# Twelve modulation products, a sooner first load and another order of the first rows in a two-block layer

## Time and profile before

| | us |
|---|---|
| median of 3 runs | 1569.6 |
| lowest and highest | 1567.91 and 1569.87 |
| the profiled execution's own time | 1573.47 |
| its span | 1571.5 |
| PE busy | 1459.9 (93%) |
| DVE busy | 1049.8 (67%) |
| POOL busy | 563.6 (36%) |
| ACT busy | 546.4 (35%) |
| DMA moved | 571.91 MB, mean 364 GB/s |

### The profile page before, as it was taken

The page is one execution under the profiler, slowest core; times in us unless marked ns, Lnnn a source line. Parts: engine busy times, 40 slices in busy tenths (PEclk is TensorE's granted clock), DMA queues, the critical chain, the costliest instruction groups (busy, mean ns, idle before and its releaser), DMA issues.

```text
span 1571.5 us, 22748 instructions
## 1 busy us (share of the span) xinstructions
PE 1459.9 (93%) x8272; PEld 1120.8 (71%) x8272; DVE 1049.8 (67%) x2170; ACT 546.4 (35%) x1128; POOL 563.6 (36%) x382
## 2 busy tenths in 40 slices
PE   8999999999999999999999999998988988888777
PEld 7999998767999999998989985444444443333333
DVE  6655376875734328998976468785858585858556
ACT  5444353363544436443134242221212121212114
POOL 2455428220344441001002234554545444444451
PEclk9999999999999999999999999999999998999999
DMA  9888958996999997999976969999999999999996
GB/s 365 312 329 317 348 217 338 315 326 241 407 372 371 376 376 294 374 398 342 362 281 226 401 244 403 404 427 427 427 427 426 427 427 427 427 427 427 426 428 267
DMA packets 99814, 571.91 MB, mean 364 GB/s; under 512 B 11536, under 2 KB 11664, under 8 KB 50448
## 3 DMA queue, kind: packets, MB, share of 16 engines
q1 hardware_dynamic: 61056, 298.15, 51.3%
q0 software_dynamic: 37520, 268.47, 40.7%
q10 hardware_dynamic: 1152, 4.16, 0.7%
HBM read 569.67 MB, written 135.27 MB: 449 GB/s over the span
## 4 chain that ended last, share of the span: by engine, by line
PE 57%; DMA 26%; DVE 6%; SPq 5%; POOL 3%; issue 2%; ACT 1%; ACTq 0%; POOLq 0%; DVEq 0%
DMA arena<-pairs,eidx 15%; PE ps L2727 10%; PE ps L2113 8%; PE ps L2112 8%; PE ps L2111 8%; DMA ring<-pairs,eidx 6%; PE ps L2504 5%; SPq L664 3%; PE ps L2200 2%; PE ps L2198 2%; PE ps L2199 2%; DMA arena<-in_ada 2%; POOL w_lo L754 2%; SPq L663 2%; PE ps L2619 2%
## 5 line engine op out<-in xcount | busy, mean ns | idle before, releaser
L2727 PE MATMUL ps<-arena 128*128 128x512 f32 x844 | 402.6, 626 | 69.1 <-ACT arena L1252 69.1
L2727 PEld LDWEIGHTS ps<-arena 128*128 128x128 f32 x844 | 165.8, 201 | 289.0 <-issue 192.8
L1965 DVE CUSTOM_DVE_ANT_0 arena<-arena 128x1024 f32<-128x1024 f32 x211 | 255.2, 1225 | 145.3 <-DMA arena<-pairs,eidx 144.1
L822 POOL DMA_INDIRECT arena<-pairs,eidx x210 | 244.3, 1163 | 257.1 <-PE ps L2727 208.4
L754 POOL TENSOR_TENSOR w_lo<-ring,w_hi 128x1024 fp32r<-128x1024 f32 x76 | 207.9, 2738 | 257.7 <-DVE w_lo L1305 171.3
L2111 PE MATMUL ps<-u_hi,w_hi 128*128 128x256 f32 (+1 forms) x912 | 259.4, 284 | 1.8 <-POOL w_lo L754 1.5
L2113 PE MATMUL ps<-u_hi,w_lo 128*128 128x256 f32 (+1 forms) x912 | 259.6, 285 | 0.0
L2112 PE MATMUL ps<-u_lo,w_hi 128*128 128x256 f32 (+1 forms) x912 | 259.2, 284 | 0.0
L842 ACT ACTIVATE w_hi<-ring 128x1024 fp32r<-128x1024 f32 x188 | 197.8, 1056 | 149.7 <-PE ps L2200 71.2
L2111 PEld LDWEIGHTS ps<-u_hi,w_hi 128*128 128x128 f32 x912 | 172.1, 189 | 3.2 <-issue 2.3
L2113 PEld LDWEIGHTS ps<-u_hi,w_lo 128*128 128x128 f32 x912 | 172.3, 189 | 0.0
(11 more groups left out here) (394 smaller groups left out, 2505.3 us busy)
## 6 DMA issues: line engine op xcount, KB each, us to landing
ring<-in_stream SPq DMA_DIRECT2D x121, 1024.0 KB, 7.0
pairs<-in_peer_u SPq DMA_DIRECT2D x128, 512.0 KB, 7.5
pairs<-in_peer_v SPq DMA_DIRECT2D x128, 512.0 KB, 8.6
arena<-in_ada SPq DMA_DIRECT2D x32, 768.0 KB, 6.4
arena<-in_stream SPq DMA_DIRECT2D x8, 1024.0 KB, 9.9
arena<-pairs,eidx POOLq DMA_INDIRECT x210, 19.7
h<-in_x_t SPq DMA_DIRECT2D x2, 544.0 KB, 4.7
ring<-in_stream SPq DMA_DIRECT2D x2, 512.0 KB, 7.1
```

Source lines behind the costliest of these rows:

```text
L822: pool.indirect_dma_start(slot_of(n), None, pairs, own).then_inc(landing(n)[0], 16)
L1965: dve.tensor_tensor_reduce(row, row, hf[:, n % HEAD_ROWS // TOPK, :], 1.0, 0.0, ALU.mult, ALU.add, dots[:, n % HEAD_ROWS:n % HEAD_ROWS + 1 ...
L2727: mm = pe.matmul(ps[:, Y_BANKS[j // TOPK] + half, :], diag[:, n % DIAGS, :], slot_of(n)[:, D + half * 512:D + half * 512 + 512], start=(hd ...
```

## The change

- **Modulation.** A tile now holds 32 of the rows for all four quarters of the columns, so a partition stands for (quarter, row), and all 32 tiles are added into one accumulator 128 x 1536 (`ada_flat`). Each addition waits for the one before. The scale needs c laid out anew: `silu_c` is 128 x 32, loaded by four small DMAs on SP from the columns in device memory, behind the first four weight pieces, and ACT's SiLU waits for them. PE sums the partitions by 12 products with a new constant `quarter` (64 columns), once, at the second feed-forward's first piece; DVE adds all 48 biases at once and makes both gains there. The products, the bias and `gain2` in the z stage are gone.
- **Second feed-forward.** SP issues the load of its first piece behind the fifth of the last eight modulation loads. ACT's high part is placed at k = 2 instead of 4, DVE's low part at m = 4 instead of 5. The last eight additions are spread: two before the first sum, one before each of the next five, one before the last.
- **First tile's squares.** DVE adds the eight squares of the first tile into one (`square_added`, seven additions of 128 x 128) between its sums, and PE makes one mean product (`first_mean`) instead of eight. The copy of the first queries goes by halves on DVE and ACT. PE's order is half query, mean, half query, the first half of the next output tile, the scores, its second half.
- **First rows.** `HALF_HEADS` has (2, 0), (2, 1), (3, 0), (3, 1), (4, 0) after groups 3, 5, 7, 9 and 11 instead of 1, 3, 5, 7 and 10. Steps 25 and 42 take the next slot in rotation, and steps 33 and 49 take their new ones. ACT does head 1's copies in group 1, behind its diagonals, and its score copy last. PE weighs two of group 1's rows ahead of head 1's scores and two behind.
- **End.** Only the first half is multiplied by `final_g` beforehand and then scaled by ACT; the second half is done by DVE in one instruction with both factors. The two halves change queues for the output.

The diff, with context cut:

```diff
...
@@ -67,13 +68,13 @@
 RING_HEADS = [4, 5]
-HALF_HEADS = {1: (2, 0), 3: (2, 1), 5: (3, 0), 7: (3, 1), 10: (4, 0), 13: (4, 1),
+HALF_HEADS = {3: (2, 0), 5: (2, 1), 7: (3, 0), 9: (3, 1), 11: (4, 0), 13: (4, 1),
               16: (5, 0), 19: (5, 1), 22: (6, 0), 25: (6, 1), 28: (7, 0), 31: (7, 1)}
...
 OUT_SLOTS = [5, 6, 7, 0]
-NEW_SLOTS = {0: 1, 1: 2, 2: 5, 3: 6, 4: 7, 5: 0, 6: 4, 7: 3, 8: TAIL_SLOT, 9: LENT_SLOT, 14: 10, 25: 8, 42: 9, 67: 11, 92: 12}
+NEW_SLOTS = {0: 1, 1: 2, 2: 5, 3: 6, 4: 7, 5: 0, 6: 4, 7: 3, 8: TAIL_SLOT, 9: LENT_SLOT, 14: 10, 33: 8, 49: 9, 67: 11, 92: 12}
 GAIN_AFTER = 33
...
@@ -114,7 +114,7 @@
 CONSTS = [("ident", P), ("mean_d", P), ("iota", TOPK), ("mean_256", P), ("mean_128", P), ("mean_64", P), ("mean_96", P),
-          ("ones", P), ("rot", P), ("cos", T), ("sin", T), ("neg_mask", P)]
+          ("ones", P), ("rot", P), ("cos", T), ("sin", T), ("neg_mask", P), ("quarter", WIDE)]
 CON = {}
...
@@ -652,8 +658,8 @@
                 sp.wait_ge(ada_step, kt * ADA_Q + (q + 3))
-                n = kt * ADA_Q + q
-                src = a["ada"][n] if isinstance(n, int) else a["ada"][bass.ds(n, 1)].rearrange("o p w -> p (o w)")
+                quarters = slice(kt * ADA_Q, kt * ADA_Q + ADA_Q) if isinstance(kt, int) else bass.ds(kt * ADA_Q, ADA_Q)
+                src = a["ada"][quarters, q * ADA_ROWS:(q + 1) * ADA_ROWS, :]
                 sp.dma_start(ada_ring[:, q % 2, :], src).then_inc(ada_in[q % 2], 16)
@@ -676,6 +682,10 @@
                 sp.dma_start(ring[:, n, :], a["stream"][n]).then_inc(landed[n], 16)
+            c_rows = a["cols"][:, COL["c"]:COL["c"] + KT].rearrange("(q r) k -> r q k", q=ADA_Q)
+            for g in range(ADA_Q):
+                own = silu_c[g * ADA_ROWS:(g + 1) * ADA_ROWS, :].rearrange("r (q k) -> r q k", q=ADA_Q)
+                sp.dma_start(own, c_rows).then_inc(c_in, 16)
@@ -695,13 +705,14 @@
             at += BEFORE_ADA
-            with sp.Fori(0, KT // 2 - 2) as kt:
-                for q in range(ADA_Q):
-                    load_ada(kt + (KT // 2 + 2), q)
-                    for n in range(ADA_BLOCKS):
-                        pair_up(kt * (ADA_Q * ADA_BLOCKS) + (at + q * ADA_BLOCKS + n))
-            at += (KT // 2 - 2) * ADA_Q * ADA_BLOCKS
-            for part, end, each in (("ffn2", "z_gate", 1), ("z_gate", "w_b", 2), ("w_b", "w_out_2", 1)):
+            for n in range(2 * ADA_Q):
+                load_ada(KT - 2 + n // ADA_Q, n % ADA_Q)
+                if n == ADA_Q:
+                    load(BASE["ffn2"], BASE["ffn2"] % RING)
+            pair_up(at)
+            load_pieces(BASE["ffn2"] + 1, BASE["z_gate"], at + 1, 1)
+            at += BASE["z_gate"] - BASE["ffn2"]
+            for part, end, each in (("z_gate", "w_b", 2), ("w_b", "w_out_2", 1)):
                 load_pieces(BASE[part], BASE[end], at, each)
...
@@ -884,7 +895,7 @@
                     act.activation(dst[:, k, 0:w], h[:, k, c], ACT.Square).then_inc(sq_done, 1)
-                    if n == 2 and k == 4:
+                    if n == 2 and k == 2:
                         piece = BASE["ffn2"]
@@ -949,7 +960,8 @@
             u_high(0)
-            act.activation(silu_c[:, :], V("c", 0, KT), ACT.Silu).then_inc(silu_c_done, 1)
+            act.wait_ge(c_in, 16 * ADA_Q)
+            act.activation(silu_c[:, :], silu_c[:, :], ACT.Silu).then_inc(silu_c_done, 1)
             ffn(0)
...
@@ -1185,8 +1197,8 @@
-                act.wait_ge(q_scaled, t + 2)
                 for e in range(2):
+                    act.wait_ge(q_scaled, 5 if t else 2 * e + 2)
                     own = qh[:, 0, e, t * P:(t + 1) * P]
@@ -1253,11 +1265,11 @@
                         tok_copy(n)
+                if g == 1:
                     for e in range(2):
                         half_head(1, e)
+                    first_gate_exp(1)
                     score_copy(1)
-                if g == 1:
-                    first_gate_exp(1)
                 if j == TOPK + (GROUP if hd == 0 else -GROUP) and hd < HEADS - 1:
@@ -1281,10 +1293,10 @@
             act.activation(fin[:, 7:8], fin[:, 5:6], ACT.Sqrt, bias=fin[:, 6:7], scale=1.0 / D).then_inc(fin_act, 1)
-            act.wait_ge(fin_step, FINAL_STEPS + 7)
-            act.activation(acc[:, 1, HALF_D:D], hf[:, 1, HALF_D:D], ACT.Copy, scale=fin[:, 9:10]).then_inc(end_act, 1)
+            act.wait_ge(fin_step, FINAL_STEPS + 6)
+            act.activation(acc[:, 1, 0:HALF_D], hf[:, 1, 0:HALF_D], ACT.Copy, scale=fin[:, 9:10]).then_inc(end_act, 1)
             act.wait_ge(end_act, 4)
-            act.dma_start(out[0, P:2 * P, HALF_D:D], acc[:, 1, HALF_D:D]).then_inc(out_done, 16)
+            act.dma_start(out[0, P:2 * P, 0:HALF_D], acc[:, 1, 0:HALF_D]).then_inc(out_done, 16)
@@ -1367,9 +1379,9 @@
                 dve.wait_ge(ada_in[q % 2], kt * 32 + (q // 2 * 16 + 16))
-                dve.wait_ge(ada_step, kt * ADA_Q + (q + 1))
-                dve.scalar_tensor_tensor(ada_acc[:, q, :], ada_ring[:, q % 2, :], silu_c[:, bass.ds(kt, 1)],
-                                         ada_acc[:, q, :], ALU.mult, ALU.add).then_inc(ada_step, 1)
+                dve.wait_ge(ada_step, kt * ADA_Q + (q + ADA_Q))
+                dve.scalar_tensor_tensor(ada_flat, ada_ring[:, q % 2, :], silu_c[:, bass.ds(q * KT + kt, 1)],
+                                         ada_flat, ALU.mult, ALU.add).then_inc(ada_step, 1)
@@ -1552,10 +1564,10 @@
                 scale_p(n)
+            ADDS_BEFORE = {0: (0, 1), 1: (2,), 2: (3,), 3: (4,), 4: (5,), 5: (6,), 7: (7,)}
             for m in range(KT):
-                for i in range(2 * m, 2 * m + 2):
-                    if i < 2 * ADA_Q:
-                        ada_add(KT - 2 + i // ADA_Q, i % ADA_Q)
+                for i in ADDS_BEFORE.get(m, ()):
+                    ada_add(KT - 2 + i // ADA_Q, i % ADA_Q)
                 if m % 2:
@@ -1563,15 +1575,19 @@
                     raw_low(2, m - 1, V("g_ffn2", m - 1))
-                if m == 5:
+                if m == 4:
                     low(1, BASE["ffn2"], BASE["ffn2"] % RING)
...
             dve.wait_ge(ada_mm, 1)
-            then(dve.tensor_tensor(ada[:, 0:24], ps[:, 1, 0:24], V("ada_b", 0, 24), ALU.add), ada_done)
+            by_quarter = "p (q j) -> p q j"
+            sums = ps[:, 1, 0:48].rearrange("p (j q) -> p q j", q=ADA_Q)
+            then(dve.tensor_tensor(ada[:, :].rearrange(by_quarter, q=ADA_Q), sums, V("ada_b", 0, 48).rearrange(by_quarter, q=ADA_Q), ALU.add),
+                 ada_done)
             then(dve.scalar_tensor_tensor(gain1[:, :], ada[:, 8:16], 1.0, V("norm1", 0, KT), ALU.add, ALU.mult), ada_done)
+            then(dve.scalar_tensor_tensor(gain2[:, :], ada[:, 32:40], 1.0, V("norm2", 0, KT), ALU.add, ALU.mult), ada_done)
             ffn(1, lambda k: gain1[:, k:k + 1])
@@ -1587,7 +1603,6 @@
-            dve.wait_ge(ada_mm, 2)
             for n in range(2 * RAW):
@@ -1597,8 +1612,6 @@
-            then(dve.tensor_tensor(ada[:, 24:48], ps[:, 1, 24:48], V("ada_b", 24, 24), ALU.add), ada_done)
-            then(dve.scalar_tensor_tensor(gain2[:, :], ada[:, 32:40], 1.0, V("norm2", 0, KT), ALU.add, ALU.mult), ada_done)
...
@@ -1782,10 +1795,14 @@
+                own = slice(t * P, (t + 1) * P)
+                if t == 0:
+                    for e in range(2):
+                        dve.wait_ge(q_mm, e + 1)
+                        dve.tensor_copy(q_shift[:, e:e + 1], ps[:, e, 0:1]).then_inc(q_scaled, 1)
+                        dve.tensor_tensor(qh[:, 0, e, own], ps[:, e, 1:1 + P], rstd[:, own], ALU.mult).then_inc(q_scaled, 1)
+                    return
                 dve.wait_ge(q_mm, 2 * t + 2)
-                if t == 0:
-                    dve.tensor_copy(q_shift, ps[:, 0:2, 0]).then_inc(q_scaled, 1)
-                own = slice(t * P, (t + 1) * P)
                 dve.tensor_tensor(qh[:, 0, :, own], ps[:, 2 * t:2 * t + 2, 1 + t * P:1 + (t + 1) * P],
@@ -1796,8 +1813,19 @@
+            def square_added(m):
+
+                first = slice(0, P)
+                dve.wait_ge(sq_done, 4 * KT + m + 1)
+                if m > 1:
+                    dve.wait_ge(tiles_added, 2 + m - 1)
+                dve.tensor_tensor(u[:, 0, first], u[:, 0, first], u[:, m, first], ALU.add).then_inc(tiles_added, 1)
+
             for m in range(KT):
                 out_added(0, m)
+                if m >= 2:
+                    square_added(m - 1)
+            square_added(KT - 1)
             tile_rstd(0)
@@ -2081,13 +2109,12 @@
                 last_half(half)
-            for half in range(2):
-                c = slice(half * HALF_D, (half + 1) * HALF_D)
-                then(dve.tensor_tensor(hf[:, 1, c], acc[:, 1, c], final_g[:, c], ALU.mult), fin_step)
+            then(dve.tensor_tensor(hf[:, 1, 0:HALF_D], acc[:, 1, 0:HALF_D], final_g[:, 0:HALF_D], ALU.mult), fin_step)
             dve.wait_ge(fin_act, 2)
...
             dve.wait_ge(end_act, 3)
-            dve.tensor_scalar(acc[:, 1, 0:HALF_D], hf[:, 1, 0:HALF_D], fin[:, 9:10], None, ALU.mult).then_inc(half_out, 1)
```

(41 more changed lines are left out.)

27 lines of the change are left out of this document (16 added, 11 removed).

## The result

The changed kernel took 1735.63 us (median of 4 runs, 1726.54 to 1739.49) for 1569.73 of the kernel before; the ratio is 1.104, 95% interval 1.101 to 1.107. One of the four runs of the kernel before took 2858.45 us; its others agree with each other to 0.2% and no trace of that run was kept. I had forecast 1558.0 with a range of 1554.5 to 1564.0. Its profiled execution took 1732.44 us with a span of 1730.6.

The account below looks back on a forecast made before the run. PE bounds until the first gather near 918 us, then DMA at 427 GB/s. Sum +0.1 - 3.2 - 2.8 - 1.7 - 3.6 - 0.4 = -11.6 us: span 1559.9, median 1558.0 us, range 1554.5 to 1564.0.

Parts of the forecast that it names:

- Start: Kernel start: larger constants add 0.1 us; the four small c loads land by 22 to 24 us, costing 0.
- The rival on the slower side: Start: c loads' 512 pieces of 32 bytes are slow and delay ACT's SiLU; 1576 us; chance 0.04.
- rival 1: After the first gather: gaps stay, 383 GB/s being the cost of starting gathers; without 3.6, 1561.6 us; chance 0.17.
- rival 3: Gathered rows 25 to 32: too few slots, so groups wait; 1571 us, or 1569; chance 0.09.
- rival 2: Second feed-forward's start: POOL's subtractions and additions hold each other, last modulation load late; 3.2 us go, 1561.2; chance 0.10.
- That each addition now waits for the one before costs nothing: Modulation additions before the second feed-forward: chaining them on one accumulator costs 0 where their load is later still.
- First tile: Second feed-forward's first tile: PE's 1.95 us wait for the first weights' low part goes; last addition at 397 to 399.
- 12 products, first place: Second feed-forward: 12 products take 2.65 us, PE takes its next weight pair at 416.75; gain 3.2 us, including the 1.95.
- Z stage: Second place of the products: 5.3 us leave PE, 2.5 return as a wait on DVE's low part; gain 2.8 us.
- First query: Before the first gather: one mean product and new PE order start the picks 1.7 us sooner; first gather near 910.1.
- First rows and end: After the first gather, 3.6 us of the 955 to 995 shortfall won; at the end, one product fewer, 0.4 us.

Follow-up runs that it names:

- the contiguous kernel: Changed kernel with modulation tiles stored as contiguous blocks, loaded with 128 rows as first dimension, not 4: 1562.27 us, ratio 0.995; again 1566.15 us, ratio 0.997.
- run 7: Changed kernel with contiguous tiles, one part undone each: first rows' order 1569.05 us; whole modulation 1567.17 us; second feed-forward's early work 1564.9 us.

## Why the prediction was wrong, point by point

**The step that failed** is the one that isn't there. The prediction costs the four c loads, the additions, the products and the moved load, and has no term for the loads of the modulation tiles; their new form was read as a matter of layout. I even stated a rule on the size of pieces for the c loads, 16 kB in all, and passed by 25 MB whose rows stayed at 6 kB but whose first dimension fell from 128 to 4. Bytes and size of pieces were unchanged, so by the figures of "Start" the load had to be free. The first dimension set how many DMA engines carried a tile, 4 of 16, and at some 25 GB/s for each the loads could not keep up. What it cost can be worked out from rows. A turn of the first loop moves two weight pieces, one copy of pairs and one tile. The additions stand 12.1 us apart in the contiguous kernel and 16.5 to 17.5 in the changed one (58.27, 75.72, 92.26):

```profile
58.27 1.82 DVE L1383 SCALAR_TENSOR_TENSOR arena<-arena,silu_c 128x1536 f32<-128x1536 f32 x1 [3.52 <-DMA arena<-in_ada]
75.72 1.82 DVE L1383 SCALAR_TENSOR_TENSOR arena<-arena,silu_c 128x1536 f32<-128x1536 f32 x1 [6.47 <-DMA arena<-in_ada]
92.26 1.82 DVE L1383 SCALAR_TENSOR_TENSOR arena<-arena,silu_c 128x1536 f32<-128x1536 f32 x1 [5.89 <-DMA arena<-in_ada]
```

The four engines carry a sixteenth of 3.15 MB and a quarter of 0.786 MB, 0.39 MB a turn, and at some 23 to 25 GB/s that is 16 to 17 us; the weight pieces have a sixteenth of their bytes on the same four engines and wait with them. The first loop has 16 such turns: from its first addition to its last are 260.2 us in the changed kernel and 166.6 in the contiguous one, 94 us more. The next eight turns have one piece, one tile and no pairs, 0.26 MB on each of the four engines, and take 82.5 us for 34.8, 48 more. The last eight tiles come 7.3 to 10.5 us apart where they were 2 to 5 apart, 59.3 us for 27.2, another 32. Together 173; 3 to 4 are won back in the gaps between, and the last addition starts at 565.5 for 395.4. That is 170 us later, and the spans differ by 171. SP's queue shows the same from the other side: issuing a tile took it 0.33 us in the median before, and takes 0.64 now and up to 4.9. One of the longer ones:

```profile
60.26 2.12 SPq L663 DMA_DIRECT2D arena<-in_ada  x1
```

**The rival on the slower side** had the right family (a load whose form makes it slow) and the wrong load. It had a chance of 0.04, and slower as a whole 0.03. The c loads cost nothing: in the changed kernel ACT's SiLU ran at 31.21, its table load at 29.92 for 29.62, and that 0.3 is the later start.

```profile
31.21 0.23 ACT L964 ACTIVATE silu_c<-silu_c 128x32 f32<-128x32 f32 x1
```

**Rivals 1 to 3** did not decide anything. The gaps went (rival 1): 426 GB/s where 383 stood. Slots did not run short (rival 3): the rate is 427 GB/s on from there. POOL's subtractions and the additions did hold each other (rival 2), but in another place, as the next point says.

**The other steps.** By the trace of the contiguous kernel the forecast times held nearly to the tenth, and up to the output projection that is luck. Two things that I had not in the sum cancel there. PE starts the projection at 370.14 for 368.21, 1.9 us late, and runs it in 27.89 us for 29.55 at a clock that stays at 1.00, 1.7 us quicker; so it ends where it ended before. The 1.9 are the step "That each addition now waits for the one before costs nothing". It does cost something where two additions follow each other. Two at 208 us took 3.54 us in the kernel before and take 5.91 now:

```profile
208.10 3.54 DVE L1371 SCALAR_TENSOR_TENSOR arena<-arena,silu_c 128x1536 f32<-128x1536 f32 x2
209.99 3.91 POOL L754 TENSOR_TENSOR w_lo<-ring,w_hi 128x1024 fp32r<-128x1024 f32 x1 [3.61 <-ACT w_hi L842]
```

```profile
208.08 5.91 DVE L1383 SCALAR_TENSOR_TENSOR arena<-arena,silu_c 128x1536 f32<-128x1536 f32 x2
209.98 2.41 POOL L765 TENSOR_TENSOR w_lo<-ring,w_hi 128x1024 fp32r<-128x1024 f32 x1 [3.61 <-ACT w_hi L853]
```

The chain has the second addition begin 0.1 to 0.2 us later, and by that behind POOL's subtraction instead of ahead of it. Before, POOL was the one that was held (3.91 us for 2.41); now DVE is, by 2.4 us, and the next sums of the tokens with it. All profiled kernels with the new modulation and the full rate of loads have the 5.91, and the one with the old modulation (run 7) has not. At 235 us this has made the kernel 1.2 us late; how it grows to 1.9 by 370 I have not followed. PE's waits from 380 to 920 us in the contiguous kernel:

```profile
PE ps L2138 <- DVE w_lo L1601: 2.5, 1, 2.5
PE ps L2138 <- issue: 1.4, 1, 1.4
PE ps L2577 <- DVE arena L1731: 0.4, 1, 0.4
```

- *First tile.* The 1.95 us wait of the earlier trace rows is gone. The last addition stood at 395.36 and ended ahead of the last sum (forecast 397 to 399), POOL's subtraction and one low part of DVE took 3.79 and 2.25 us side by side, inside the cover.
- *12 products, first place.* Forecast: 2.65 us of products, then a wait of 1.4, PE on the next pair at 416.75. Measured: 24 records, a wait of 1.38, 416.89.
- *Z stage.* Forecast: a new wait of 2.5 and 5.9 us won in all so far. Measured: 2.55, and 621.88 - 616.26 = 5.6.

```profile
416.89 0.36 PE L2138 MATMUL ps<-u_hi,w_hi 128*128 128x256 f32 x1 [1.38 <-issue]
...
616.26 0.36 PE L2138 MATMUL ps<-u_hi,w_hi 128*128 128x256 f32 x1 [2.55 <-DVE w_lo L1601]
```

- *First query.* Forecast 1.7, first gather near 910.1. Measured: PE's sequence starts at 899.14 for 904.74 and the picks at 905.89 for 912.95, so 7.06 - 5.60 = 1.5, and the first gather is issued at 910.60 for 917.66.
- *First rows and end.* Forecast 4.0 together. Measured: the spans differ by 11.7, the first gathers by 7.1, so 4.6. DVE's wait of 5.70 for the second gelu is gone, and the stretch that answers to 952 to 992 is full:

```profile
910.60 1.03 POOL L833 DMA_INDIRECT arena<-pairs,eidx  x1 [4.66 <-DVE eidx L1969]
...
945.00:985.00 40.00, 38.21 (x107) 19.09 (x106) 37.19 (x107) 11.01 (x26) 22.56 (x18) 1.00 1.01 426
```

Of this 2.7 are the order of the rows, by the pair of traces in run 7, where I had 3.6; the other 1.9 lie in the end and between traces, and no run parts them. The sum of -11.6 stands against -11.7 of the spans. The medians moved by less, 9.3 and 4.4. The profiled execution of the kernel before was 3.9 us above its median, while those of the contiguous kernel, 1561.57 and 1561.65, were at or below theirs; so the sum compared one slow execution with fast ones, and taking the 3.9 off the result as if it belonged to both was too generous. At least 1.7 of the 11.7 are the stretch at 1.2 GHz that the one trace of the kernel before has and the two of the contiguous kernel have not.

## What to carry to other kernels

When a load's pattern changes, count its dimensions and not only its bytes and the size of its pieces: here the first dimension set how many of the 16 DMA engines took it, and which partitions each form wrote together went with how long a packet took. A low share of busy DMA engines together with engines that wait for DMA is the sign; share times 16 gives the number of engines, and dividing the rate by it tells whether each is at the 25 to 26 GB/s that it had here. Before a difference of a few us between two traces is put down to an edit, take out the stretches with a granted clock of 0.5: of three differences here, of 2.4 to 6.0 us, 1.5 to 2.5 us each were clock. Here the cure was to lay the tiles out in device memory as they are loaded, which keeps the gains of the change and costs nothing on the chip.

## What I had not expected of the hardware

- A load of 4 x 32 x 1536 ran on four DMA engines (share 0.26, 106 GB/s), and as they serve every other load too, 25 MB in such tiles cost 160 us, even though the engines as a whole were idle for a quarter of the time (share 0.74 from 48 to 157 us).
- Eight engines on eight groups of 16 partitions moved 122 GB/s, 15 each, hardly more than four engines on groups of 32 (106, 25 each). Why the four kept their rate is open.
- Sixteen engines on 16 groups of 8 partitions cost 30 us against the same bytes as 128 rows (1600.4 and 1599.6 for 1570.5 and 1571.0), whether the groups stood 55 or 197 kB apart.
- Four DMAs to 32 neighbouring partitions each: 1607; to every fourth partition: 1568. A 6 kB packet took 433 ns in the first and 234 in the second.
- A delay of under 0.2 us decided which of DVE and POOL was held by the other, and cost DVE 2.4 us at 208 us.
- Stretches of 3.4 and 6.8 us at 1.2 GHz came and went between profiled kernels in code that was the same, each worth 1.7 to 2.5 us where PE was the path.
